# The end of a two-layer trunk step: last combination by column halves, gated sums on GpSimd and TensorE, one sum on ScalarE

## The reference, cut to what matters

```
y  = sum over experts of gates[:, e] * swiglu(h, wg[e], wu[e], wd[e])
x  = layer_norm(ALPHA * x + gate * y) * ln_g + ln_b        # gate: one row for context, one for latents
```

## Time and profile before

| | |
|---|---|
| median of 3 runs | 1333.41 us (1333.41, 1333.41, 1337.09) |
| the profiled execution's own time | 1337.3 us |
| its span in the trace | 1335.4 us |
| TensorE matmul busy | 1278.3 us (96%) |
| VectorE busy | 715.0 us (54%) |
| ScalarE busy | 521.6 us (39%) |
| GpSimd busy | 131.2 us (10%) |

### The profile page before, as it was taken

How to read it: one execution, slowest core, us unless ns; L and a number is a source line. 1 busy time by engine, 2 the same in 40 slices (tenths; PEclk the granted TensorE clock), 3 DMA queues, 4 the chain that set the end, 5 groups by cost and what they waited for, 6 DMA issues and landing times.

```text
span 1335.4 us, 17338 instructions
## 1 busy us (share of the span) xinstructions
PE 1278.3 (96%) x6503; PEld 959.3 (72%) x6504; DVE 715.0 (54%) x1026; ACT 521.6 (39%) x632; POOL 131.2 (10%) x119
## 2 busy tenths in 40 slices
PE   4999999999999989999999999999999999999994
PEld 2555449999999964677646886765467878888882
DVE  1101456334234252555335777743256788888888
ACT  0101025233233242234202746533136666777772
POOL 0420003200000033000000010100102021202020
PEclk8999999999999989899998789999999999999997
DMA  9986386424324184720405666859989899999993
GB/s 365 351 340 247 107 319 190 158 95 161 122 94 157 47 320 144 263 78 24 173 0 194 243 228 257 294 193 341 352 317 338 293 338 357 383 366 385 362 358 142
DMA packets 125356, 317.10 MB, mean 237 GB/s; under 512 B 12931, under 2 KB 47078, under 8 KB 124774
## 3 DMA queue, kind: packets, MB, share of 16 engines
q1 hardware_dynamic: 119264, 295.00, 60.7%
q0 software_dynamic: 5744, 21.07, 5.1%
q10 hardware_dynamic: 278, 0.10, 0.0%
HBM read 306.37 MB, written 9.76 MB: 237 GB/s over the span
## 4 chain that ended last, share of the span: by engine, by line
PE 89%; DVE 5%; DMA 3%; issue 1%; SPq 1%; ACT 1%; DVEq 0%; ACTq 0%
PE ps L2546 10%; PE ps L2547 10%; PE ps L2548 10%; PE ps L2244 8%; PE ps L2246 8%; PE ps L2245 8%; PE ps L2209 7%; PE ps L2552 7%; PE ps L2146 6%; PE ps L2336 3%; DMA sb_ring<-in_ev_w_in 2%; PE ps L2106 2%; PE ps L2438 1%; PE ps L2080 1%; DVE sb_expert_lo L1753 1%
## 5 line engine op out<-in xcount | busy, mean ns | idle before, releaser
L1753 DVE TENSOR_TENSOR sb_expert_lo<-sb_expert_raw,sb_expert_hi 128x1792 fp32r<-128x1792 f32 (+1 forms) x210 | 334.1, 1646 | 85.0 <-PE ps L2552 73.7
L1201 ACT CAST sb_expert_hi<-sb_expert_raw 128x1792 fp32r<-128x1792 f32 (+1 forms) x210 | 283.4, 1392 | 117.3 <-PE ps L2548 78.4
L2546 PE MATMUL ps<-sb_expert_hi,sb_expert_x 128*128 128x448 f32 x448 | 166.9, 373 | 4.5 <-DVE sb_expert_lo L1753 2.5
L2547 PE MATMUL ps<-sb_expert_lo,sb_expert_x 128*128 128x448 f32 x448 | 165.3, 369 | 0.0
L2548 PE MATMUL ps<-sb_expert_hi,sb_expert_x 128*128 128x448 f32 x448 | 165.0, 368 | 0.0
L2244 PE MATMUL ps<-sb_split_acts,sb_split_weights 128*128 128x384 f32 x352 | 118.0, 335 | 0.4 <-issue 0.4
L2246 PE MATMUL ps<-sb_split_acts,sb_split_weights 128*128 128x384 f32 x352 | 117.9, 335 | 0.0
L2245 PE MATMUL ps<-sb_split_acts,sb_split_weights 128*128 128x384 f32 x352 | 117.7, 334 | 0.0
L2546 PEld LDWEIGHTS ps<-sb_expert_hi,sb_expert_x 128*128 128x128 f32 x448 | 85.2, 190 | 20.1 <-issue 12.7
L2548 PEld LDWEIGHTS ps<-sb_expert_hi,sb_expert_x 128*128 128x128 f32 x448 | 85.0, 190 | 7.2
L2547 PEld LDWEIGHTS ps<-sb_expert_lo,sb_expert_x 128*128 128x128 f32 x448 | 85.1, 190 | 7.0
(11 more groups left out here) (339 smaller groups left out, 1835.5 us busy)
## 6 DMA issues: line engine op xcount, KB each, us to landing
sb_expert_raw<-in_moe_w_gate SPq DMA_DIRECT2D x128, 448.0 KB, 5.6
sb_expert_raw<-in_moe_w_up SPq DMA_DIRECT2D x128, 448.0 KB, 7.0
sb_expert_raw<-in_moe_w_down SPq DMA_DIRECT2D x112, 512.0 KB, 7.3
sb_ring<-in_ada_w SPq DMA_DIRECT2D x14, 3072.0 KB, 17.7
sb_ring<-in_ffn_w_gate SPq DMA_DIRECT2D x44, 256.0 KB, 3.8
sb_ring<-in_ffn_w_up SPq DMA_DIRECT2D x44, 256.0 KB, 4.7
sb_ring<-in_ffn_w_down SPq DMA_DIRECT2D x22, 512.0 KB, 6.3
sb_ring<-in_ev_w_in SPq DMA_DIRECT2D x4, 2048.0 KB, 15.4
```

Source lines behind the costliest of these rows:

```text
L1201: nc.scalar.copy(EHI[piece.h][:, 0:w], ERAW[:, r, 0:w]).then_inc(e_hi, 1)
L1753: V.tensor_tensor(ELO[r][:, 0:w], ERAW[:, r, 0:w], EHI[piece.h][:, 0:w].bitcast(F32), ALU.subtract)\
L2546: first = mm(out, lh, rh, start=start, stop=False)
L2547: mm(out, lh, rl, start=False, stop=False)
```

## The change

The weights and all passes stay as they are. From the last down projection on:

- SP loads the three YG first, behind the last weight piece, and GB after them; the signal `sums_room` is gone.
- GpSimd waits for GB, issues LG and LB, and multiplies YG by the gate row in place for groups 1 and 2 (`sums_gated`).
- VectorE does so for group 0 only, and updates X of group 0 only. It also makes `SCALED`, the identity times ALPHA.
- The last three pieces of the down projection are taken first for bank 4, then for bank 5; `yd` is raised for each bank, and YV is made in halves of 512 columns, both gate rows of a half after one another.
- TensorE adds the gated sums of groups 1 and 2 in PSUM, by a product with the identity, and for group 2 also ALPHA * X, by a product with `SCALED`. `summed(1)` now multiplies X by ALPHA.
- ScalarE takes the third group's sum from PSUM with its accumulator and writes X (`sum_ready`); VectorE forms its mean behind `scaled(1)`.

```diff
@@ SP @@
-            tokens_split(sp, (more, 0), 0)
-            sp.dma_start(GB[:, :, :], gate_rows[1, 2:4, :].partition_broadcast(P)).then_inc(gates_back, 16)
-            sp.wait_ge(sums_room, 1)
             sp.wait_ge(y_stored, nth((more, 0), 16, 16 * (len(SECOND) - 1)))
             for g in range(NG):
                 sp.dma_start(YG[:, g, :], expert_sums[g * P:(g + 1) * P, :]).then_inc(y_got[g], 16)
+            tokens_split(sp, (more, 0), 0)
+            sp.dma_start(GB[:, :, :], gate_rows[1, 2:4, :].partition_broadcast(P)).then_inc(gates_back, 16)
@@ GpSimd @@
-            pool.wait_ge(y_got[NG - 1], 16)
+            pool.wait_ge(gates_back, 16)
             pool.dma_start(LG[:, :], ln_g[1, 1].partition_broadcast(P)).then_inc(lnp_in, 16)
             pool.dma_start(LB[:, :], ln_b[1, 1].partition_broadcast(P)).then_inc(lnp_in, 16)
+            for g in range(1, NG):
+                pool.wait_ge(y_got[g], 16)
+                pool.tensor_tensor(YG[:, g, :], YG[:, g, :], GB[:, 1, :], ALU.mult).then_inc(sums_gated, 1)
@@ ScalarE @@
-            for g in range(NG):
+            for g in range(NG - 1):
                 squares(g, NG + g, WR[:, 1, 0:D])
+            act.wait_ge(comb_ps, NG)
+            nc.scalar.activation(X[:, NG - 1, :], PS[:, 6:8, :].rearrange("p a n -> p (a n)"), ACT.Identity,
+                                 accum_out=SM[:, 27 + NG:28 + NG]).then_inc(sum_ready, 1)
+            squares(NG - 1, 2 * NG - 1, WR[:, 1, 0:D])
@@ VectorE @@
+            V.tensor_scalar(SCALED, ident, ALPHA, None, ALU.mult).then_inc(one_hot_ready, 1)
             for c in range(4, EB):
                 expert_low(e_last(more, c), "d")
             dve.wait_ge(gates_back, 16)
-            def before_last(g):
-
-                dve.wait_ge(y_got[g], 16)
-                dve.wait_ge(x_full, NG * (2 * DEPTH - 2) + g + 1)
-                ch(V.tensor_tensor(T[:, :], YG[:, g, :], GB[:, min(g, 1), :], ALU.mult))
-                ch(V.scalar_tensor_tensor(X[:, g, :], X[:, g, :], ALPHA, T[:, :], ALU.mult, ALU.add))
-
-            before_last(0)
-            before_last(1)
-            dve.wait_ge(yd, seen((more, 0)))
-            for v in range(2):
-                V.scalar_tensor_tensor(YV[:, v, :], PS[:, 4:6, :].rearrange("p a n -> p (a n)"), ROWW[:, 2, 1:2], GB[:, v, :],
-                                       ALU.mult, ALU.mult).then_inc(y_gated, 1)
+            dve.wait_ge(y_got[0], 16)
+            dve.wait_ge(x_full, NG * (2 * DEPTH - 1))
+            ch(V.tensor_tensor(YG[:, 0, :], YG[:, 0, :], GB[:, 0, :], ALU.mult))
+            ch(V.scalar_tensor_tensor(X[:, 0, :], X[:, 0, :], ALPHA, YG[:, 0, :], ALU.mult, ALU.add))
+            for q in range(2):
+                half = slice(q * 512, (q + 1) * 512)
+                dve.wait_ge(yd, seen((more, 0)) + q)
+                for v in range(2):
+                    V.scalar_tensor_tensor(YV[:, v, half], PS[:, 4 + q, :], ROWW[:, 2, 1:2], GB[:, v, half],
+                                           ALU.mult, ALU.mult).then_inc(y_gated, 1)
...
-            before_last(2)
             summed(0)
             summed(1)
             dve.wait_ge(lnp_in, 48 * (2 * DEPTH - 1) + 32)
             scaled(0)
-            summed(2)
             scaled(1)
+            dve.wait_ge(sum_ready, 1)
+            V.tensor_scalar(SM[:, 15 + NG:16 + NG], SM[:, 27 + NG:28 + NG], -1.0 / D, None, ALU.mult).then_inc(mean_ready, 1)
             scaled(2)
@@ TensorE @@
-            down((more, -1), 1, [e_last(more, b) for b in range(EB)], lambda: None, False)
-            pe.wait_ge(one_hot_ready, 1)
-            for g in range(NG):
-                pe.wait_ge(y_gated, min(g, 1) + 1)
-                for h in range(2):
-                    last = mm(PS[:, (0, 2, 6)[g] + h, :], OH[:, g * P:(g + 1) * P], YV[:, min(g, 1), h * 512:(h + 1) * 512],
-                              start=True, stop=True)
-                last.then_inc(comb_ps, 1)
+            LATE = 3
+            def last_down(p, pieces):
+                b = blocks_of(p)[0]
+                def product(j, q):
+                    cols, half, r, hi = slice(b.home(j), b.home(j) + b.n), slice(q * 512, (q + 1) * 512), pieces[j].r, pieces[j].h
+                    return three_products(PS[:, b.down[0] + q, :], (EHS[1][0][:, cols], EHS[1][1][:, cols]),
+                                          (EHI[hi][:, half], ELO[r][:, half]), False, j == EB - 1)[1]
+                hidden_split(pe, p, 1, 0)
+                for j in range(EB - LATE):
+                    piece_ready(pieces[j])
+                    product(j, 0)
+                    product(j, 1).then_inc(e_used, 1)
+                for j in range(EB - LATE, EB):
+                    piece_ready(pieces[j])
+                    last = product(j, 0)
+                last.then_inc(yd, 1)
+                for j in range(EB - LATE, EB):
+                    last = product(j, 1)
+                last.then_inc(yd, 1)
+            def sums_part(g, q):
+                if q == 0:
+                    pe.wait_ge(sums_gated, g)
+                if g == NG - 1:
+                    mm(PS[:, 6 + q, :], SCALED, X[:, g, q * 512:(q + 1) * 512], start=True, stop=False)
+                mm(PS[:, (0, 2, 6)[g] + q, :], ident, YG[:, g, q * 512:(q + 1) * 512], start=(g < NG - 1), stop=False)
+            def last_part(g, q):
+                v = min(g, 1)
+                pe.wait_ge(y_gated, 2 * q + v + 1)
+                return mm(PS[:, (0, 2, 6)[g] + q, :], OH[:, g * P:(g + 1) * P], YV[:, v, q * 512:(q + 1) * 512],
+                          start=(g == 0), stop=True)
+            last_down((more, -1), [e_last(more, b) for b in range(EB)])
+            pe.wait_ge(one_hot_ready, 2)
+            last_part(0, 0)
+            sums_part(1, 0)
+            last_part(0, 1).then_inc(comb_ps, 1)
+            sums_part(1, 1)
+            last_part(1, 0)
+            last_part(1, 1).then_inc(comb_ps, 1)
+            for q in range(2):
+                sums_part(2, q)
+                last = last_part(2, q)
+            last.then_inc(comb_ps, 1)
```

More of the change, by code:

```diff
@@ L410, in build @@
         YV = SCR[:, 8 * EW + D:8 * EW + 3 * D].rearrange("p (v n) -> p v n", v=2)
+        SCALED = T[:, 2 * TOK:2 * TOK + P]
         TW = MS[:, 700:700 + 3 * NE * NG].rearrange("p (e g c) -> p e g c", e=NE, g=NG)
@@ L423, in build @@
             lg_ps first_hot hkt_ps hk d_ready ex_ready m_ready pos_ps tab_ready pos_ready
-            gu_ps esil eh t_ps yd ysb sums_room gates_back one_hot_ready y_gated comb_ps mp_ready disp_ps xe_done h_stored y_stored pick_ps pick_sb x_got rows_zero gate_passed y_full mean_ready sq_ready
+            gu_ps esil eh t_ps yd ysb gates_back sums_gated sum_ready one_hot_ready y_gated comb_ps mp_ready disp_ps xe_done h_stored y_stored pick_ps pick_sb x_got rows_zero gate_passed y_full mean_ready sq_ready
             gates_t gates_out x_full hi_done lo_done w_used hx_hi hx_lo fh_hi fh_lo xe_hi eht_hi eht_lo
@@ L433, in build @@
          pt_ready, o_ps, o_ready, lg_ps, first_hot, hkt_ps, hk, d_ready, ex_ready, m_ready, pos_ps, tab_ready, pos_ready,
-         gu_ps, esil, eh, t_ps, yd, ysb, sums_room, gates_back, one_hot_ready, y_gated, comb_ps, mp_ready, disp_ps, xe_done, h_stored, y_stored, pick_ps, pick_sb, x_got,
+         gu_ps, esil, eh, t_ps, yd, ysb, gates_back, sums_gated, sum_ready,  one_hot_ready, y_gated, comb_ps, mp_ready, disp_ps, xe_done, h_stored, y_stored, pick_ps, pick_sb, x_got,
          rows_zero, gate_passed, y_full, mean_ready, sq_ready, gates_t, gates_out, x_full, hi_done, lo_done, w_used, hx_hi, hx_lo, fh_hi, fh_lo, xe_hi, eht_hi, eht_lo,
@@ L1997, in _ @@
                 expert_low(e_last(more, c), "d")
-            V.tensor_copy(ROWW[:, 2, :], ROWW[:, 1, :]).then_inc(sums_room, 1)
+            ch(V.tensor_copy(ROWW[:, 2, :], ROWW[:, 1, :]))
             expert_low(e_last(more, 3), "d")
-            dve.wait_ge(sums_room, 1)
             dve.wait_ge(disp_ps, seen((more, 0), 1))
@@ L2028, in summed @@
                 at = (0, 2, 6)[g]
-                ch(V.scalar_tensor_tensor(x, PS[:, at:at + 2, :].rearrange("p a n -> p (a n)"), 1.0, x, ALU.mult, ALU.add,
+                ch(V.scalar_tensor_tensor(x, x, ALPHA if g else 1.0, PS[:, at:at + 2, :].rearrange("p a n -> p (a n)"), ALU.mult, ALU.add,
                                           accum_out=SM[:, 28 + g:29 + g]))
```

## The result

The changed kernel took 1344.24 us, median of seven runs (1340.55 to 1345.49); the kernel before, in seven runs beside it, 1337.09 (1331.6 to 1339.34). The ratio is 1.0056, 95% interval 1.0034 to 1.0077: slower by 0.56%, some 7 us. I had forecast -0.5 us, a range up to 1337.8, and 0.13 for slower by over 0.3%. The prediction was wrong, and in sign as well.

What follows compares the result with a forecast made beforehand. VectorE's list and TensorE's second `comb_ps` were taken to bound the tail; 1326.9 + 1.5 + 3.43 + 3.06 = 1334.9 against 1335.4, -0.5 us, so a median of 1332.9, range 1330.9 to 1337.8.

Steps and rivals of the forecast that it cites:

- What bounds the tail: After the last down projection two chains count: VectorE's list and TensorE's second `comb_ps`, for which `summed(1)` waits.
- the end counted from the second signal: From TensorE's second `comb_ps`, forecast at 1318.8, through `summed(1)`, the `scaled` steps and last store to 1334.9.
- new wait for the squares: Before the last `scaled`, VectorE forms the mean and idles for ScalarE's squares: 1.5 us, eating the 1.38 saved.
- GB: Gate rows, now last of four loads, seen about 1309.5, so VectorE's first gated product starts 2 us later.
- GpSimd beside VectorE: Group 0's gated product and x update take turns with GpSimd's two products; the update itself takes 1.2 us.
- the tie: VectorE's x update and GpSimd's first product ready together at about 1310.8; VectorE taken first, the opposite given 0.26.
- TensorE's chain: Combination behind the down projection: starts at 1312.8, six products of 0.88 us up to the second `comb_ps` at 1318.8.
- one rival: TensorE's clock falls after its idle: four records at 0.85 for 0.44 cost 1.7 us; end +1.2, chance 0.12.
- The sum: Whole tail: 1326.9 + 1.5 + 3.43 + 3.06 = 1334.9 against 1335.4, a gain of 0.5 us; chance 0.40.
- GpSimd wins the tie, with a fall: VectorE's x update waits 2.4 us for GpSimd's product and TensorE's clock falls after longer idle: +3.0 us, chance 0.18.
- no reading of the tail reaches -4: Even with gate rows early and engines independent, the end isn't before 1332.6, as added products and squares cancel savings.
- the half clock that lasts: TensorE's combination stays at half clock; with all twelve products slow the end is 1345; chance 0.03.

Runs made afterwards that it cites:

- e6: e3 with the third group's mean formed on ScalarE instead of VectorE; one profiled execution, tail 20.8 us against 22.3.
- e1: Changed kernel with GpSimd's two products waiting for VectorE's x update of group 0; median 1337.45 us, ratio 1.0004 to the kernel before.
- e4: Changed kernel with GpSimd waiting for its own first product before starting the second; one profiled execution, tail 26.7 us against the changed kernel's 30.7.
- e2: Changed kernel with the gate rows loaded ahead of the three loads of sums, as before; ratio 1.0020 to the kernel before.
- e5: Changed kernel with seven products of constants filling TensorE's idle before the combination; one profiled execution, tail 27.3 us against the changed kernel's 30.7.
- e7: Changed kernel: gate rows first, GpSimd's products behind VectorE's first gated product, x update behind YV, third mean on ScalarE; 1332.83 us, ratio 0.9972 to before.
- e3: Changed kernel with gate rows loaded first and GpSimd's products behind VectorE's x update of group 0; 1336.52 us, ratio 0.9993 to the kernel before.

## Why the prediction was wrong

**What bounds the tail, and the end counted from the second signal: right.** I had 16.1 us from that signal to the end; it was 16.0. The new wait for the squares was 1.31 us with a 0.15 us mean (forecast 1.5 together), and e6 shows that it was worth 1.5.

**GB.** The place was right, and that VectorE has no cover for it. The size was about right for this execution (the product started 1.1 us ahead of the down projection's end, I had 1.7) and too high for most, 2.3 to 2.6.

**GpSimd beside VectorE: this step failed.** I took the engines to hold and be held in turns, and had 1.2 us for the update, or 3.6 if it lost the tie. It took 5.98: it was held through both of GpSimd's products. That GpSimd held it is shown by e1 (1.23 us with the products behind it); that the tie was lost my rival had at 0.26. That it was held twice no reading of mine had. A wait of GpSimd for its own first product brings the turn back (e4, 3.70). I had read turns from the earlier trace rows, and there one turn has such a wait ahead of it (`ch`, between L851 and L852) and the other, like e2's, has none. So the wait is enough but isn't the whole rule. In both turns without it the GpSimd instruction ahead had been held by VectorE (3.27 and 3.09 us), and in the changed kernel and e5 it had not; whether this decides stays open.

With e1 the step's price can be read. Of the 7.2 us of tail between the two, 1.2 are the changed execution's late gate rows. The other 6.0 are the step: 4.75 of the update and about 2.3 of half clock that follows the idle, less 0.8 that TensorE in e1 waits for the later product of group 1 (its second product starts 1.66 us behind the first instead of 0.86) and 0.2 in handovers.

**TensorE's chain.** The price of a product was right: 0.86 at full clock (0.88 in the sum), and six stand ahead of the signal. That they come to 5.2 us in a row is seen in e7. The clock fell to 0.50 as one rival had it, but for five records at 0.85 us in place of 0.43 instead of four: 2.3 us by e5, where the rival had 1.7. From the first combination to the signal I had 6.0, it was 7.6.

**The sum.** In tails: forecast 23.7, measured 30.7. In times, I had counted from a median of 1333.41 us in three runs; the seven beside the changed kernel gave 1337.09, spread from 1331.6 to 1339.34 and not on two levels. That doesn't save the forecast: with 3.7 us added the range would end at 1341.5. In tails again, the late start of the combination is 5.5 of the 7.0 (0.6 gate rows, 4.75 update, the rest handovers), the half clock less the wait that it covers 1.6; behind the signal the difference is 0.1 us.

**The rivals.** "GpSimd wins the tie, with a fall" was the mechanism that came, at +3.0; its terms for both the hold and the fall were too small. My statement that no reading of the tail reaches -4 stands for this order of instructions (e3, both holds gone, gains 1.9). e7 gains 4.4, of which the third mean on ScalarE is 1.5 (e6) and the moved update with GpSimd's earlier start 1.0. I had no reading on the other side between +3.0 and the half clock that lasts, since I had not asked whether two GpSimd instructions in a row let VectorE in between.

## What to carry to other kernels

A product moved to GpSimd can hold a VectorE instruction that reads two operands from SBUF, and two in a row can hold it through both. Put them beside VectorE instructions that read one operand from PSUM, behind a signal of VectorE's (e1, e7), or let GpSimd wait for its own product in between (e4). When an operation is seen to take turns in one place, look at what each instruction waited for, and which engine had been held before, before its price is carried to another place. If a hold makes TensorE idle, count the half-clock records behind it as well, and compare short ends by the tail from a common event, not by the span.

## What the runs showed of the hardware

- Two GpSimd products 128x1024, the second without a wait for the first, kept a VectorE instruction with two SBUF operands out for 4.66 us (changed kernel; 4.71 in e5). It got in behind the first where GpSimd waited for its own product (e4, 0.08 us between them), and also without such a wait where the first had been held by VectorE (e2; and at 228 us). In the changed kernel, e2, e4, e5 and e7 it ended 1.09 or 1.10 us behind the GpSimd instruction that held it. The Trainium skill (GPSIMD Engine Reference, Specifications) names the contention; these runs agree, and show in part how the turns fall.
- The YV instructions (one operand in PSUM, one in SBUF) took 2.73 us for four with and without GpSimd at work.
- A start shown first isn't enough: a VectorE update shown as begun 0.23 us ahead of GpSimd's product was held (changed kernel, e4 and e5), a product begun 0.38 us ahead (e2) ran its 1.22 us, and GpSimd's took 3.09.
- TensorE's idle of 1.22 and 2.02 us was followed by no fall of the granted clock, 2.87, 3.53, 4.14 and 7.12 us by a fall to 0.50. Products of constants in the idle kept it at 1.00 (e5).
